# Feed-forward of a hybrid decoder step: the opening block of each token run computed with eight plain block products instead of a seven-product scheme, its combined activations formed during that block

## The reference

```python
h2 = rms_norm(x, norm2_g) * (1 + sc2) + sh2
x = x + g2 * (jnp.square(jax.nn.relu(h2 @ w_ff1)) @ w_ff2)
```

## Time and profile before

| | |
|---|---|
| median of 3 runs (lowest to highest) | 2892.45 us (2891.02 to 2900.97) |
| the profiled execution | 2897.07 us |
| its span in the profile | 2894.9 us |
| PE busy in the span | 2694.6 us, 93% |
| POOL, DVE, ACT busy | 47%, 56%, 42% |
| first feed-forward matmul | 1427.82 us after the span's start |

### The profile page before, as it was taken

One profiled execution on the slowest core, in us unless ns is written; L12 is line 12 of the kernel. 1 busy time (PEld: TensorE's weight loads), 2 busy tenths in 40 slices (PEclk: granted clock), 3 DMA queues, 4 the chain that ended last, 5 costly groups with the idle time before them and its releaser, 6 DMA issues.

```text
span 2894.9 us, 46504 instructions
## 1 busy us (share of the span) xinstructions
PE 2694.6 (93%) x16282; PEld 2309.3 (80%) x16282; DVE 1628.3 (56%) x3810; ACT 1228.7 (42%) x3105; POOL 1362.4 (47%) x987
## 2 busy tenths in 40 slices
PE   6899989979999967999589999989999998999999
PEld 2678848856666634687389999989999998999998
DVE  3158889856666624787654444474444447444444
ACT  3334313546666622465433433443433344334432
POOL 0000000019997000665366765676666676657664
PEclk6999989989999989999799999999999999999999
DMA  7566626647654378466214224225222423413222
GB/s 271 193 217 229 207 98 231 215 144 206 186 181 147 122 267 306 138 204 207 74 59 131 86 90 137 74 93 178 77 88 78 132 88 118 156 59 104 87 73 77
DMA packets 312171, 421.91 MB, mean 146 GB/s; under 512 B 27050, under 2 KB 241434, under 8 KB 305790
## 3 DMA queue, kind: packets, MB, share of 16 engines
q1 hardware_dynamic: 289394, 328.43, 34.9%
q0 software_dynamic: 5072, 81.05, 7.9%
q10 hardware_dynamic: 17476, 9.47, 1.1%
HBM read 342.28 MB, written 148.74 MB: 170 GB/s over the span
## 4 chain that ended last, share of the span: by engine, by line
PE 39%; DVE 4%; issue 3%; POOL 2%; DMA 2%; ACT 1%; SPq 0%; DVEq 0%; POOLq 0%; ACTq 0%
PE ff_u_ps L2700 13%; PE ff_u_ps L2701 13%; PE ff_u_ps L2702 13%; POOL ff_w_lo L2396 2%; DMA gluT<-in_w_ff_dram 2%; DVE ff_h_lo L2535 1%; DVE ff_wT L2545 1%; POOL ff_a_lo L2411 0%; DVE ff_wT L2544 0%; ACT ff_w_hi L2446 0%; PE ff_out_ps L2695 0%; DVE gluT L2522 0%; DVE ff_wT L2547 0%; DVE gluT L2525 0%; DVE ff_y L2589 0%
## 5 line engine op out<-in xcount | busy, mean ns | idle before, releaser
L2396 POOL TENSOR_TENSOR ff_w_lo<-gluT,ff_w_hi 128x512 fp32r<-128x512 f32 x336 | 459.1, 1374 | 270.9 <-ACT ff_w_hi L2446 270.5
L2700 PE MATMUL ff_u_ps<-ff_a_hi,ff_w_hi 128*128 128x352 f32 (+1 forms) x1536 | 497.3, 324 | 29.8 <-DVE ff_y L2589 17.7
L2701 PE MATMUL ff_u_ps<-ff_a_lo,ff_w_hi 128*128 128x352 f32 (+1 forms) x1536 | 496.3, 323 | 0.0
L2702 PE MATMUL ff_u_ps<-ff_a_hi,ff_w_lo 128*128 128x352 f32 (+1 forms) x1536 | 495.9, 323 | 0.0
L2700 PE MATMUL ff_u_ps<-ff_h_hi,ff_w_hi 128*128 128x352 f32 (+1 forms) x1344 | 435.9, 324 | 36.0 <-POOL ff_h_lo L2405 28.6
L2702 PE MATMUL ff_u_ps<-ff_h_hi,ff_w_lo 128*128 128x352 f32 (+1 forms) x1344 | 431.5, 321 | 0.0
L2701 PE MATMUL ff_u_ps<-ff_h_lo,ff_w_hi 128*128 128x352 f32 (+1 forms) x1344 | 431.2, 321 | 0.0
L2589 DVE SCALAR_TENSOR_TENSOR ff_y<-ff_u_ps,modT,ff_y 128x352 f32<-128x352 f32 (+2 forms) x336 | 187.8, 570 | 355.7 <-PE ff_u_ps L2702 355.6
L2396 POOL TENSOR_TENSOR ff_w_lo<-ff_wT,ff_w_hi 128x512 fp32r<-128x512 f32 x192 | 263.6, 1374 | 243.1 <-ACT ff_w_hi L2446 175.9
L2446 ACT ACTIVATE ff_w_hi<-gluT 128x512 fp32r<-128x512 f32 x336 | 207.3, 625 | 308.1 <-PE ff_u_ps L2702 277.0
L2700 PEld LDWEIGHTS ff_u_ps<-ff_a_hi,ff_w_hi 128*128 128x128 f32 x1536 | 293.1, 191 | 34.7 <-DVE ff_y L2589 19.8
(11 more groups left out here) (308 smaller groups left out, 5267.5 us busy)
## 6 DMA issues: line engine op xcount, KB each, us to landing
gluT<-in_w_ff_dram SPq DMA_DIRECT2D x192, 512.0 KB, 5.0
out_new_k_sample_dram<-in_cache_k_dram POOLq DMA_DIRECT2D x8, 4088.0 KB, 15.6
out_new_v_sample_dram<-in_cache_v_dram POOLq DMA_DIRECT2D x8, 4088.0 KB, 16.4
dwq<-in_w_ada_dram SPq DMA_DIRECT2D x32, 512.0 KB, 7.3
gluT<-in_cache_k_dram SPq DMA_DIRECT2D x16, 1024.0 KB, 11.8
sa_vn<-in_cache_v_dram SPq DMA_DIRECT2D x16, 1024.0 KB, 19.1
mx_acc<-acc_d SPq DMA_DIRECT2D x16, 768.0 KB, 7.9
vu_x_in<-in_x_prompt_dram SPq DMA_DIRECT2D x16, 512.0 KB, 4.8
```

The source lines that it names most:

```text
L2396: pool.tensor_tensor(slot_view(w_lo, s), src, slot_view(w_hi, s).bitcast(F32), ALU.subtract).then_inc(w_lod, 1)
L2700: pe.matmul(out, w_hi[:, s % WR, w], hi, start=first, stop=False, skip_group_check=more)
L2701: pe.matmul(out, w_hi[:, s % WR, w], lo, start=False, stop=False, skip_group_check=more)
L2702: return pe.matmul(out, w_lo[:, s % WR, w], hi, start=False, stop=last, skip_group_check=more)
```

## The change

In blocks 0, 8 and 16 (`is_plain`) the up phase does not use the seven-product scheme. Each pair computes its eight block products directly: four weight slots per pair (8 up slots per block, not 14), each used for two products, one for each token half (16 products, 192 matmuls). There are four PSUM groups per pair, and ACT reads each with a relu straight into `z` (`plain_relu`). These blocks need no weight sums, and of the activations only four operands: A11, A21, A12, A22. A21 is kept in the place of S1 (operand 4).

The head of a run makes only those four (`h_high` and `h_low` for g = 0 to 3: 16 copies on ACT, 8 subtractions each on DVE and POOL). The sums S2, S3, S4 are formed inside the opening block (`s_sums`, 4 sums and 3 lows on DVE per slice k, with `s_high` on ACT, 3 per k), in `wT`, which is free there. S1 needs the place of A21 and so is formed in that block's down phase (`s1_sums`, `s1_high`, `s1_low`), before and after `accumulate` 4 to 7. Activation pieces are loaded in ten groups of four per run (40 DMAs) where there were four groups (16 DMAs). The residual rows of runs 0 and 1 use two buffers in place of four. The `t_sums` for the block after an opening block stand after `accumulate` 9, not 4.

```diff
-            UP, DN = 14, 16
+            DN = 16
+            PAIR_SLOTS = [4 if b % BLKS == 0 else 7 for b in range(NB_ALL)]
+            PAIR_STEPS = [8 if b % BLKS == 0 else 7 for b in range(NB_ALL)]
+            PAIR_BANKS = [4 if b % BLKS == 0 else 3 for b in range(NB_ALL)]
...
             def x1_row(j):
-                if jj % 4 < 2:
-                    return x1_own[0:n, jj % 4]
-                return x1_lent[0:n, (jj % 4 - 2) * D:(jj % 4 - 1) * D]
+                if run == NR - 1 and jj >= 2:
+                    return x1_lent[0:n, (jj - 2) * D:(jj - 1) * D]
+                return x1_own[0:n, jj % 2]
...
-            FIN = {(0, 1): 0, (0, 3): 1, (0, 5): 2, (1, 1): 3, (1, 4): 4, (1, 6): 5}
+            FIN = {0: 0, 1: 1, 6: 2, 7: 3, 12: 4, 13: 5}
...
                 # sync
+                        if blk == 0 and t == 2:
+                            load_h(run, 4)
+                            load_h(run, 5)
+                        if blk == 0 and t == 3:
+                            if run:
+                                store(last)
+                                store(last + 1)
+                                load_x1(last + 2)
+                                load_x1(last + 3)
+                            load_h(run, 6)
+                            if run:
+                                store(last + 2)
+                                store(last + 3)
+                                load_x1(last + 4)
+                                load_x1(last + 5)
+                            load_h(run, 7)
...
+                        if blk == 1 and t == 1:
+                            load_h(run, 8)
+                            load_h(run, 9)
...
                 # scalar, up phase
+                            if is_plain(b):
+                                if o % 2:
+                                    plain_relu(e + o - 1)
+                                    plain_relu(e + o)
+                                high(SLOT0[b] + i + WR)
+                                if o % 2:
+                                    a_high(e + o - 1)
+                                    a_high(e + o)
+                                    s_high(run, 2 * j + o // 2)
+                                continue
...
                 # vector
-                    s_sums(0, 0)
-                    t_sums(0)
-                    for k in range(4):
-                        s_low(0, k)
-                        if k < 3:
-                            s_sums(0, k + 1)
+                    h_low(0, 0)
+                    h_low(0, 2)
...
+                        if is_plain(b):
+                            for k in range(4):
+                                if run and k < 3:
+                                    finish((run - 1) * TR + 2 * k)
+                                    finish((run - 1) * TR + 2 * k + 1)
+                                s_sums(run, k)
...
                         for d in range(DN):
                             accumulate(b, d)
-                            if ahead and d % 2 and d < 8:
-                                s_low(run + 1, d // 2)
-                                if d < 7:
-                                    s_sums(run + 1, d // 2 + 1)
-                            if d == 4 and b + 1 < NB_ALL:
-                                t_sums(2 * b + 2)
+                            if blk == BLKS - 1 and run < NR - 1 and d in (1, 5):
+                                h_low(run + 1, d // 2)
+                            if is_plain(b) and d == 3:
+                                s1_sums(run)
+                            if is_plain(b) and d == 7:
+                                s1_low(run)
+                            if blk < BLKS - 1 and d == (9 if is_plain(b) else 4):
+                                t_sums(b + 1, 0)
...
                 # tensor
+                            if is_plain(b):
+                                for n in range(2):
+                                    name, bank = (("A11", 0), ("A21", 1), ("A12", 0), ("A22", 1), ("A11", 2), ("A21", 3), ("A22", 3), ("A12", 2))[2 * o + n]
...
+                                        mm = three(u_ps[g % 6][:, 0:w], s, kk, h_hi[:, h, kk, 0:w], h_lo[:, h, kk, 0:w],
+                                                   o % 2 == 0 and kk == 0, o % 2 == 1 and kk == 3)
```

More of the change, by code:

```diff
@@ L2191, in build, with is_plain, pair_number, plain_number @@
             DORD = [(0, 1), (1, 1), (0, 0), (1, 0)] + [(k, c) for k in range(2, KT) for c in range(2)]
+            def is_plain(b):
+                return b % BLKS == 0
+            def pair_number(b, j):
+                return (b - b // BLKS - 1) * 2 + j
+            def plain_number(b, j):
+                return b // BLKS * 2 + j
+            def locate(s):
+                b = next(n for n in range(NB_ALL) if SLOT0[n + 1] > s)
+                return b, s - SLOT0[b]
             def unit_slot(U):
@@ L2386, in _ @@
                     for i in range(4):
-                        sp.wait_ge(out_s[i], 16 * NR * (2 if i < 2 else 1))
+                        sp.wait_ge(out_s[i], 16 * sum(store_slot(j) == i for j in range(len(flat))))
                 @block.gpsimd
@@ new lines, in s_high, with s1_high @@
+                    def s_high(run, k):
+                        w = RUNS[run][1]
+                        for m, (o, n) in enumerate(((3, 2), (1, 1), (6, 3))):
+                            act.wait_ge(s_d, 16 * run + 4 * k + m + 2)
+                            act.activation(h_hi[:, o, k, 0:w], wT[:, n, 0:w], ACT.Copy).then_inc(shh_d, 1)
+                    def s1_high(run):
+                        w = RUNS[run][1]
+                        act.wait_ge(u_pe, up_done(run * BLKS))
+                        for k in range(4):
+                            act.wait_ge(s1_d, 4 * run + k + 1)
+                            act.activation(h_hi[:, 4, k, 0:w], z[k][:, 0:w], ACT.Copy).then_inc(s1h_d, 1)
@@ L2506, in _, with h_low @@
                                 h_high(run + 1, k)
-                            high(b * SLOTS + UP + k + WR)
+                            if blk == 0 and k == 2:
+                                s1_high(run)
+                            high(SLOT0[b] + up_slots(b) + k + WR)
                 @block.vector
                 def _(v):
+                    def h_low(run, g):
+                        w = RUNS[run][1]
+                        o = {0: 0, 2: 2}[g]
+                        for n in range(4):
+                            i = h_pieces(run, g)[n]
+                            h_ready(v, run, g, n)
+                            v.wait_ge(ahh_d, 16 * run + 4 * g + n + 1)
+                            v.tensor_tensor(h_lo[:, o, n, 0:w], h_raw[:, i, 0:w], h_hi[:, o, n, 0:w].bitcast(F32), ALU.subtract).then_inc(ahl_v, 1)
@@ L2537, in t_sums @@
-                    def t_sums(q):
-                        U = (q // 2) * 4 + q % 2
-                        b11, b21, b12, b22 = raw_up(q)
-                        raw_ready(v, U)
-                        if q:
-                            low_wait(v, unit_slot(((q - 1) // 2) * 4 + (q - 1) % 2) + 5)
+                        a11, a21, a22, a12 = (h_raw[:, i, 0:w] for i in h_pieces(run, 4 + k))
+                        st = [wT[:, n, 0:w] for n in range(4)]
+                        for n in range(4):
+                            h_ready(v, run, 4 + k, n)
@@ new lines, in s1_low, with t_sums @@
+                    def s1_low(run):
+                        w = RUNS[run][1]
+                        for k in range(4):
+                            v.wait_ge(s1_d, 4 * run + k + 1)
+                            v.wait_ge(s1h_d, 4 * run + k + 1)
+                            v.tensor_tensor(h_lo[:, 4, k, 0:w], z[k][:, 0:w], h_hi[:, 4, k, 0:w].bitcast(F32), ALU.subtract).then_inc(s1l_d, 1)
+                    def t_sums(b, j):
+                        q = pair_number(b, j)
+                        b11, b21, b12, b22 = raw_up(b, j)
+                        raw_ready(v, b * 4 + j)
+                        if j:
+                            v.wait_ge(w_lod, unit_slot(b * 4) + 6)
+                        elif b % BLKS == 1:
+                            v.wait_ge(shl_d, 12 * (b // BLKS + 1))
+                        else:
+                            v.wait_ge(w_lod, unit_slot((b - 1) * 4 + 1) + 6)
@@ L2617, in _ @@
                             if j == 0:
[L2618 to L2621 removed]
+                                t_sums(b, 1)
+                            v.wait_ge(u_pe, product_done(b, j, 1))
                             v.wait_ge(p1_d, q + 1)
@@ L2732, in _ @@
                             mm.then_inc(u_pe, 1)
-                            if blk == 0 and run and (i // 7, o) in FIN:
-                                finish((run - 1) * TR + FIN[i // 7, o])
                         def down(d, fs, first, last):
```

457 lines of the change are left out of this document (238 added, 219 removed).

## The result

The changed kernel takes **2875.2 us** (median of 4 runs, 2874.97 to 2880.02), beside 2892.86 us before (4 runs, 2891.02 to 2900.97): ratio 0.9937, 95% interval 0.9925 to 0.9949. The profiled execution after took 2880.02 us (span 2878.2).

What follows compares the result with a forecast made beforehand. The stage was taken as bound by its number of matmuls, apart from a few places losing time. Terms 10.3 - 23.6 + 2.9 - 28.1 + 13.8 + 1.5 = -23.2 us gave 2869 us from the 2892.45 median; range 2853 to 2887 us.

Steps and rivals of the forecast that it cites:

- head, to the end of up 0: First up phase ends 20.0 us earlier: 23.6 us of gain less 3.6 us for added matmuls.
- down 0: After the first up phase, the last activation low comes late: 1.4 us stall, 1.5 us lower clock, +2.9 us.
- down 7 and 15: Down phases before runs 1 and 2: both excesses, 14.3 and 13.8 us, go, -28.1 us.
- up 8 and 16: Opening up phases of runs 1 and 2: added matmuls, plus 1.3 us stall and 0.7 us clock each at a finish.
- down 8 and 16: Down phases opening runs 1 and 2: PE waits 2.9 us for the late `a_low`, plus 2.0 us of clock, each.
- blocks 1, 9 and 17: Blocks holding a cache copy: later weight lows cost +0.5 us each, +1.5 us.
- I book no stall: Late pieces 8 and 9 for S1 and moved weight sums stay inside PE's six-group lead; without that cover, 7 us per opening.
- Rival 4: DVE becomes the bound of the opening blocks, sums waiting out POOL: 36 us more, 2905 us; chance 0.08.
- the rule of the Trainium skill weighed above: DVE and POOL share a port pair, locked exclusively for a whole instruction, so every sum may wait out a POOL operation.
- Rival 1: The openings run clean, without stalls of 2.9, 13.8 and 1.5 us: -41.4 us, 2851 us; chance 0.12.

Runs made afterwards that it cites:

- the narrow boundary: Kernel before the change, with DVE's sums and their lows for runs 1 and 2 made 8 columns wide: 2871.48 us, ratio 0.9933.
- kernel (a): Changed kernel with ACT's last activations ahead of the third round's sum copies and the fourth round of sums moved into the down phase: 2870.8 us, ratio 0.9922.
- kernel (d): Changed kernel with the opening blocks' activations split ahead of the weight slot on ACT and POOL: 2866.2 us, ratio 0.9900.
- the narrow sums: Changed kernel with DVE's sums and their lows 8 columns wide in the second and third token run: 2869.71 us, ratio 0.9919.
- kernel (a+d): Changed kernel with sum copies behind the activations, fourth sum round in the down phase, and activations ahead of weight slots; no load moved: 2875.4 us, ratio 0.9935.
- moves (a) to (d): Changed kernel with sum copies and fourth round later, pieces 4, 5, 8 and 9 loaded earlier, and activations ahead of weight slots: 2858.2 us, ratio 0.9864.

## Why the prediction came out as it did

The range held the time and the sign was right; the median is 6.2 us above the forecast. The stage came out 2.6 us from its forecast, and that is in part luck: the errors of its steps come to +9.1 and -6.5 us. Step by step, from the two profiles:

| step | forecast | measured |
|---|---|---|
| head, to the end of up 0 | -20.0 | -22.6 |
| down 0 | +2.9 | +8.3 |
| down 7 and 15 | -28.1 | -27.6 |
| up 8 and 16 (3.6 + 3.1 of matmuls, 4.0 of stalls) | +10.7 | +10.0 |
| down 8 and 16 | +9.8 | +7.4 |
| blocks 1, 9 and 17 | +1.5 | +0.7 |
| all other phases | 0 | +3.2 |
| the stage | -23.2 | -20.6 |

- **The head** was right in mechanism, and 2.6 us better than booked. Counted from ACT's first operation, POOL's lows of A21 ended at 7.0 us where 7.1 was expected, its last lows of A22 at 14.4 where 16.0 was, since SP asked for their pieces 1.4 us sooner. PE went on with the last 144 matmuls 1.7 us sooner and took 23.3 us for them, not 24.2. Up 0 is 5.9 us over the 30.6 us that 192 matmuls take.
- **Down 0 is the step that failed.** "A stall of 1.4 us and 1.5 us at the lower clock" left DVE's sums of block 0 out: I priced ACT's and POOL's chain after the last product, and did not ask when the sums ahead of it on ACT could be there. The landing time of 2.8 us was the median of eight pieces that the kernel before asked for in two groups of four; here eight pieces in a row stood behind a weight unit and took 5.1 to 6.2 us each. The first sum needs the first four of them, and started 8.0 us after the first was issued. Then each sum took 1.03 to 1.62 us where a POOL operation ran beside it, and 0.51 to 0.52 where none did. In the last three rounds of block 0 the twelve sums came to 16.3 us instead of 6.1 (12 x 0.51). PE waited 5.0 us for `ff_a_lo` and 0.7 for `ff_y` and spent the rest at a granted clock of 0.91.
- **Down 7 and 15** came off in full, and the narrow boundary shows why: DVE's operation time was 10.5 of 14.3 us.
- **Up 8 and 16.** The turn-round of the `finish` rows stalled PE 1.1 and 1.5 us where 1.3 was expected, at the fourth `finish`. Of the 2 us booked for a block 1.6 and 1.7 came, though the clock stayed at 1.00, where 0.7 us had been booked for a lower one.
- **Down 8 and 16.** The expected wait for the last `a_lo` came, 1.8 and 1.9 us instead of 2.9, and a second for `ff_y`, 0.5 and 0.7 us, that I had not booked. The reason given, copies of the sums ahead of the last activations on ACT, is part of it: with those copies moved (kernel (a)) the wait for `ff_a_lo` at down 8 fell to 0.4 us, but `ff_y` took 1.4. The weight slot ahead of the activations (kernel (d)) and DVE's time (the narrow sums) count as well: each, removed alone, takes over half of the loss at down 8.
- **"I book no stall" for S1** was nearly right for the change, whose `ff_y` waits sum to 1.9 us, but it is a cover with nothing to spare: DVE stands 9 us there, and in kernel (a+d) it cost 2.2 to 2.9 us an opening.
- **Blocks 1, 9 and 17** are near their forecast by luck. The later weight lows were to cost in the down phases, and these changed by -2.5, -1.1 and +0.9 us. Down 1 did get shorter: it is 35.3 us in both profiles with the old opening and 32.2 to 33.6 in all eleven with the new one; why is open. Down 9 and 17 vary by more than they changed. What was lost lies in the up phases, +3.4 us, in the waits put down to "issue".
- **The other phases** were no term at all. They now run in 27.02 or 27.32 and 30.56 or 30.80 us instead of mostly 26.96 and 30.56: 3.2 us over the stage, cause open.

Rival 4 named the right mechanism for one block of three. The mean of the 48 sums in the openings is 0.88 us (42.1 us / 48), inside the 0.7 to 0.9 given; in the last three rounds of block 0 it is 1.35, above the 1.3 from which that rival decides if it holds everywhere. It did not: in block 8 POOL is idle beside most of the sums, and eleven of its first twelve sums took 0.51 to 0.53 us. By the rule of the Trainium skill weighed above ("SBUF — State Buffer", SBUF: two separate sides, Reading the diagram) a sum waits out a POOL operation that began before it. The trace agrees: 0.51 us with POOL idle at 1454.98, 1.62 at 1459.39, where the second of two POOL operations was under way that end at 1460.63; the sum ends 0.38 us after it.

Rival 1, the clean openings, was put at 41.4 us of gain. The kernel with moves (a) to (d) has its stage 37.2 us shorter than before, with down 0, 8 and 16 clean, the 3 us of the slower pace left, and losses of 1.6 and 2.0 us left in up 8 and up 16. So the sum of rival 1 was about right, and nearly all of it could be had.

## What to carry to other kernels

- When work moves into another phase, follow every fixed queue behind it and date its inputs: first the load, with what is queued ahead of it, then each engine. Down 0 was lost where several such queues met.
- Late work in several queues does not add up; the largest idle time in a view need not be worth anything alone (15.8 us of DVE waiting, removed for nothing). Undo the causes together, then take them away one by one.
- Put what the next phase's first matmuls need ahead of what only refills buffers, on each engine of the chain: moving the weight slot behind the activations on two queues gave 1.8 us in one block.

## What the hardware showed beyond that

- **A DVE sum waits for POOL to the end.** Of the 48 sums of the openings in the change, 22 began while a POOL operation was running, and each of them ended 0.36 to 0.39 us after that operation's end; with POOL idle a sum takes 0.49 to 0.53 us. POOL pays too: in the last three rounds of block 0 its `ff_a_lo` operations took 1.20 to 1.23 us, in the steady blocks 0.95 (median).
- **Two paces of the same matmuls at full clock.** Up phases of 168 matmuls take 26.96, 27.02 or 27.32 us, down phases of 192 take 30.56 or 30.80, with the granted clock at 1.00 in all. Two executions of kernels with the same TensorE program don't agree on which block has which. Both phases of a steady block share the pace: in the changed kernels 27.02 always goes with 30.56 and 27.32 with 30.80. The narrow run, 26.3 and 29.4 us, hardly varies.
- **Earlier stages drift.** The same instructions reached ACT's first `ff_w_hi` between 1417.6 and 1428.2 us, a spread of 10.6 us, half of the effect under study. Count from an event inside the changed stage.
- **Down phases beside a cache copy vary by 3 us.** Those of blocks 5, 9 and 13 took 31.8 to 35.0 us in no order that follows the edits (down 5 was 32.87 in the change and 34.69 with all moves).
- **The granted clock makes such a difference too.** Down 16 took 34.13 us at 0.95 in the change, and 32.56 at 1.00 in the kernel that differs by one idle wait.
